# Hybrid diffusion trunk on one core: the second layer's last two modulation units from its mixer into its routing, its second gate's rows loaded during the expert blocks

## What is computed

```python
def adaln(cvec, w_ada_l, b_ada_l):
    m = jax.nn.silu(cvec) @ w_ada_l + b_ada_l
    return jnp.split(m[:, None, :], 6, axis=-1)
...
for l in range(DEPTH):
    sh1, sc1, g1, sh2, sc2, g2 = adaln(c, w_ada[l], b_ada[l])
    h = modulate(rmsnorm(xs, norm1_w[l]), sh1, sc1)
    mix = mixer_latent(h, ...)
    xs = xs + g1 * mix
    h = modulate(rmsnorm(xs, norm2_w[l]), sh2, sc2)
    xs = xs + g2 * moe_ffn(h, w_router, router_bias, w_gate[l], w_up[l], w_down[l])
```

## Time and profile before

| | us |
|---|---|
| median of three runs | 757.26 (756.87 to 758.19) |
| the profiled execution | 757.27, span 755.5, mean granted clock 0.996 |

### The profile page before, as it was taken

How to read it: one execution, slowest core, us unless ns; L and a number is a source line. 1 busy time by engine, 2 the same in 40 slices (tenths; PEclk the granted TensorE clock), 3 DMA queues, 4 the chain that set the end, 5 groups by cost and what they waited for, 6 DMA issues and landing times.

```text
span 755.5 us, 10417 instructions
## 1 busy us (share of the span) xinstructions
PE 723.2 (96%) x3950; PEld 354.8 (47%) x3950; DVE 328.2 (43%) x880; ACT 215.8 (29%) x491; POOL 141.4 (19%) x234
## 2 busy tenths in 40 slices
PE   5899999999999999999999999999999899999995
PEld 3357553346445534433344755435644653443332
DVE  2022625647635552312471253474853556231157
ACT  2210145745024101011322024574602310110132
POOL 4146032220110100101102502313011011010112
PEclk9999999999999999999999999999999999999998
DMA  8999335997208799999896233497430379999962
GB/s 315 354 325 364 113 118 194 386 377 296 113 8 349 305 414 414 423 418 424 315 387 244 92 111 119 164 387 306 175 113 14 126 316 410 422 421 421 423 251 84
DMA packets 65655, 207.95 MB, mean 275 GB/s; under 512 B 8089, under 2 KB 8961, under 8 KB 53315
## 3 DMA queue, kind: packets, MB, share of 16 engines
q1 hardware_dynamic: 54936, 179.86, 61.5%
q10 hardware_dynamic: 5547, 16.12, 5.5%
q0 software_dynamic: 5120, 11.28, 4.4%
HBM read 199.92 MB, written 12.88 MB: 282 GB/s over the span
## 4 chain that ended last, share of the span: by engine, by line
PE 77%; DVE 8%; DMA 8%; ACT 3%; issue 2%; POOL 1%; SPq 1%; POOLq 0%; ACTq 0%; DVEq 0%
PE bank L2413 15%; PE bank L2297 11%; PE bank L2040 8%; PE bank L2428 7%; PE bank L1984 6%; PE bank L2097 5%; PE bank L1905 5%; DMA arena<-in_w_up_dram 3%; PE bank L2026 3%; DMA ring<-in_w_ada_dram 2%; PE bank L2404 2%; PE bank L2142 2%; PE bank L2130 2%; DMA arena<-y_exp,y_idx 2%; PE bank L2389 1%
## 5 line engine op out<-in xcount | busy, mean ns | idle before, releaser
L2413 PE MATMUL bank<-ring,work 128*32 128x512 f32 (+1 forms) x640 | 114.2, 595 | 1.3 <-DMA arena<-in_w_up_dram 1.3
L2413 PEld LDWEIGHTS bank<-ring,work 128*32 128x32 f32 (+1 forms) x640 | 33.3, 120 | 73.1 <-issue 72.0
L1739 DVE COPY xs_tok<-bank 128x256 f32<-128x256 f32 x20 | 8.5, 424 | 134.7 <-PE bank L2420 134.7
L2428 PE MATMUL bank<-ring,xs_tok 128*64 128x512 f32 (+2 forms) x320 | 65.7, 597 | 1.0 <-DVE xs_tok L1739 1.0
L2040 PE MATMUL bank<-arena,ring 128*128 128x384 f32 x192 | 62.2, 486 | 0.0
L2413 PE MATMUL bank<-arena,work 128*64 128x512 f32 (+1 forms) x128 | 56.9, 597 | 0.0
L848 POOL DMA_INDIRECT gather_at<-h_rows,idx x18 | 18.2, 1011 | 173.1 <-PE bank L2404 130.7
L1905 PE MATMUL bank<-ring,cpad 128*32 128x512 f32 x384 | 49.7, 603 | 0.7 <-DMA ring<-in_w_ada_dram 0.7
L2040 PEld LDWEIGHTS bank<-arena,ring 128*128 128x128 f32 x192 | 36.5, 190 | 25.0
L1984 PE MATMUL bank<-ring,arena 128*128 128x512 f32 x96 | 42.8, 598 | 0.9 <-DVE arena L1281 0.6
L2297 PE MATMUL bank<-ring,arena 128*128 128x512 f32 x96 | 43.6, 597 | 0.0
(11 more groups left out here) (384 smaller groups left out, 1100.6 us busy)
## 6 DMA issues: line engine op xcount, KB each, us to landing
ring<-in_w_ada_dram SPq DMA_DIRECT2D x48, 1024.0 KB, 10.1
ring<-in_w_down_dram SPq DMA_DIRECT2D x28, 1024.0 KB, 10.6
ring<-in_w_gate_dram SPq DMA_DIRECT2D x24, 1024.0 KB, 7.2
ring<-in_w_up_dram SPq DMA_DIRECT2D x24, 1024.0 KB, 10.7
ring<-in_w_in_dram SPq DMA_DIRECT2D x15, 1024.0 KB, 14.9
ring<-in_w_out_dram SPq DMA_DIRECT2D x8, 1024.0 KB
arena<-in_w_gate_dram SPq DMA_DIRECT2D x8, 1024.0 KB
arena<-in_w_up_dram SPq DMA_DIRECT2D x8, 1024.0 KB
```

The lines of the kernel that those rows point to most:

```text
L2413: last = mm(bank[b][at:at + n, :].rearrange("p (i f) -> p i f", i=2), rows_T[:, kt * P + at:kt * P + at + n], gate_up_of(s)[:, kt, :, :], ...
L2428: last = mm(bank[5 + hf][at:at + n, :], hidT[:, b, f * P + at:f * P + at + n], w[:, f, hf * 512:(hf + 1) * 512], start=f == 0, stop=f == 1)
```

## The change

ADA_CUT gets a further cut at 22, so that group 4 of layer 1 has six units (16 to 21) and a new group 5 has units 22 and 23, which hold g2 of layer 1. ADA_GAP becomes a pair, one group for each layer's routing. In ORDER the out units of layer 1 go ahead of the two units. FILL of layer 1 loses its places (2, "end"), "states", ("scan", 0) and ("scan", 2), one half unit each. In layer 1's routing the units are put where three and four constant products were, and ada_columns where two of four were. GATES gets a third entry: in layer 1, g1 is transposed, stored and loaded ahead of the output products as before; g2 is transposed by PE behind hid_of(2), stored by ACT in block 2, and loaded in block 4, and DVE waits for it only ahead of result_gated(0). The store of layer 1's states goes ahead of moe unit 2, not of unit 4.

```diff
@@ -43,8 +43,8 @@
-ADA_CUT = (2, 4, 14, 16, 24)
-ADA_MIX, ADA_GAP = (2, 4), 3
+ADA_CUT = (2, 4, 14, 16, 22, 24)
+ADA_MIX, ADA_GAP = (2, 4), (3, 5)
 ADA_COL = [0, 2, 1, 3, *range(4, 24)]
@@ -58,8 +58,7 @@
     ORDER += [("out", OUT_U * _l + j) for j in range(OUT_U)]
-    if _l == 0:
-        ORDER += [("ada", j) for j in range(*ADA_CUT[ADA_GAP - 1:ADA_GAP + 1])]
+    ORDER += [("ada", j) for j in range(*ADA_CUT[ADA_GAP[_l] - 1:ADA_GAP[_l] + 1])]
     MOE_AT.append(len(ORDER))
@@ -293,7 +292,7 @@
         ada_part = qT[:, 1, :, :].rearrange("p a c -> p (a c)")
-        part_of = lambda i: qkv_flat[:, 0:512] if i == ADA_GAP else ada_part
+        part_of = lambda i: qkv_flat[:, 0:512] if i in ADA_GAP else ada_part
         modT = sb("modT", DEPTH, 48, 2)
@@ -308,8 +307,10 @@
         exp_at = lambda k: 4 if k == 1 else min(2 * k + 3, 24)
-        GATES = (((0, 0), (0, 1)), ((1, 0), (1, 1)))
-        gate_cols = ada_part[0:2 * KT, 0:2 * P].rearrange("r (n c) -> r n c", n=2)
+        GATES = (((0, 0), (0, 1)), ((1, 0),), ((1, 1),))
+        LAST_GATE = len(GATES) - 1
+        gate_cols = [v[0:2 * KT, 0:2 * P].rearrange("r (n c) -> r n c", n=2)
+                     for v in (ada_part, ada_part, qkv_flat[:, 2 * DM:])]
         epst = sb("epst", 4)
@@ -461,7 +462,8 @@
         ADA_BANK = 7
-        bank_of = lambda i: bank[5 if i == ADA_GAP else ADA_BANK]
+        bank_of = lambda i: bank[5 if i in ADA_GAP else ADA_BANK]
+        gates_psum = bank[ADA_BANK][0:2 * KT, 2 * P:4 * P]
         MIX_BANK = (0, 6, 6)
@@ -488,7 +490,7 @@
                  (1, 0, "after"): 1, (1, 2, "after"): 1, (1, 3, "after"): 1, (1, "end"): 1,
-                 (2, 0, "ahead"): 1, (2, 2, "ahead"): 1, (2, "end"): 1, "states": 1, ("scan", 0): 1, ("scan", 2): 1})
+                 (2, 0, "ahead"): 1, (2, 2, "ahead"): 1})
         assert [sum(_f.values()) for _f in FILL] == [ADA_PARTS * (ADA_CUT[_i] - ADA_CUT[_i - 1]) for _i in ADA_MIX]
@@ -623,7 +625,7 @@
                 for pair, k in MOE_UNITS:
-                    if (pair, k) == ((0, 1), SPLIT)[l]:
+                    if (pair, k) == ((0, 1), (1, 0))[l]:
                         states_stored(l)
@@ -955,25 +957,25 @@
-            def gates_stored(l):
-                n = len(GATES[l])
-                k = 2 * l
-                act.wait_ge(s_gt, l + 1)
-                act.activation(gate_cols[:, 0:n, :],
-                               bank[ADA_BANK][0:2 * KT, 0:n * P].rearrange("r (n c) -> r n c", n=n),
+            def gates_stored(i):
+                n = len(GATES[i])
+                act.wait_ge(s_gt, i + 1)
+                act.activation(gate_cols[i][:, 0:n, :], gates_psum[:, 0:n * P].rearrange("r (n c) -> r n c", n=n),
                                ACT.Copy).then_inc(s_gtc, 1)
-                act.wait_ge(s_gtc, l + 1)
+                act.wait_ge(s_gtc, i + 1)
+                k = 2 * GATES[i][0][0] + GATES[i][0][1]
                 for g in range(2):
-                    dma(gate_dram[k:k + n, g].rearrange("n b c -> b n c"), gate_cols[g::2, 0:n, :]).then_inc(s_gst, 16)
-            def gates_loaded(l):
+                    dma(gate_dram[k:k + n, g].rearrange("n b c -> b n c"), gate_cols[i][g::2, 0:n, :]).then_inc(s_gst, 16)
+            def gates_loaded(i):
+                l = GATES[i][0][0]
                 act.wait_ge(s_out, 16 * STORES * (l + 1))
...
                 act.wait_ge(s_yoff, 4 * (l + 1))
-                act.wait_ge(s_gst, 32 * (l + 1))
-                for w in range(2):
+                act.wait_ge(s_gst, 32 * (i + 1))
+                for _l, w in GATES[i]:
                     for g in range(2):
@@ -1130,8 +1132,7 @@
                     rows_stored(t)
-                if l == 0:
-                    ada_rows(ADA_GAP)
+                ada_rows(ADA_GAP[l])
@@ -1162,6 +1163,10 @@
                         silu(e + 1, (e + 1) % 2)
+                    if l == DEPTH - 1 and e == 2:
+                        gates_stored(LAST_GATE)
+                    if l == DEPTH - 1 and e == 4:
+                        gates_loaded(LAST_GATE)
                     if e == NB - 2:
@@ -1738,13 +1743,13 @@
-                dve.wait_ge(s_gate[1], 32 * (l + 1))
+                if l < DEPTH - 1:
+                    dve.wait_ge(s_gate[1], 32 * (l + 1))
                 one_hots(ROWS_AT, LISTS[1][1])
...
                 one_hots(*LISTS[2])
-                if l == 0:
-                    modulation(ADA_GAP)
+                modulation(ADA_GAP[l])
                 hidden(0, 0)
@@ -1762,6 +1767,8 @@
                 weighted(0)
+                if l == DEPTH - 1:
+                    dve.wait_ge(s_gate[1], 32 * (l + 1))
                 result_gated(0)
@@ -1952,12 +1959,12 @@
-            def gate_rows(l):
-                pe.wait_ge(s_mod, ADA_MIX[l] + 1)
-                for k, (ll, w) in enumerate(GATES[l]):
-                    last = tr(bank[ADA_BANK][0:2 * KT, k * P:(k + 1) * P],
-                              modT[:, ll, 24 * w + 16:24 * w + 24, :].rearrange("p b g -> p (b g)"), ident[:, :])
+            def gate_rows(i, group):
+                pe.wait_ge(s_mod, group + 1)
+                for k, (l, w) in enumerate(GATES[i]):
+                    last = tr(gates_psum[:, k * P:(k + 1) * P],
+                              modT[:, l, 24 * w + 16:24 * w + 24, :].rearrange("p b g -> p (b g)"), ident[:, :])
                 last.then_inc(s_gt, 1)
@@ -2330,7 +2337,7 @@
                 projected(0, 0)
-                gate_rows(l)
+                gate_rows(l, ADA_MIX[l])
                 y_turned(2)
@@ -2345,10 +2352,7 @@
                 pe.wait_ge(s_oc, 2 * NT * (l + 1))
-                if l == 0:
-                    ada(ADA_CUT[ADA_GAP] - 1)
-                else:
-                    clock_kept(5, 3)
+                ada(ADA_CUT[ADA_GAP[l]] - 1)
                 norm_transposes(k, 2)
@@ -2356,10 +2360,7 @@
                 back(2)
-                if l == 0:
-                    ada(ADA_CUT[ADA_GAP])
-                else:
-                    clock_kept(5, 4)
+                ada(ADA_CUT[ADA_GAP[l]])
@@ -2392,12 +2393,14 @@
                 pe.wait_ge(s_btc, 6 * l + 2)
-                clock_kept(4, 4)
+                if l == DEPTH - 1:
+                    ada_columns(ADA_GAP[l])
+                clock_kept(4, 4 if l == 0 else 2)
                 pe.wait_ge(s_btc, 6 * (l + 1))
...
                 if l == 0:
-                    ada_columns(ADA_GAP)
+                    ada_columns(ADA_GAP[l])
@@ -2451,8 +2454,8 @@
                     pe.wait_ge(s_yc, 2 * b + (2 * NB * l + 2))
-                    if l == 0 and b == 0:
-                        pe.wait_ge(s_mod, ADA_GAP + 1)
+                    if b == 0:
+                        pe.wait_ge(s_mod, ADA_GAP[l] + 1)
                     for p in pairs_of(b):
@@ -2508,6 +2511,8 @@
                     hid_of(b)
+                    if l == DEPTH - 1 and b == 2:
+                        gate_rows(LAST_GATE, ADA_GAP[l])
                     if b + 2 < NB:
```

## The result

The changed kernel took 760.17 us (median of 9 runs, 758.1 to 761.73) where the kernel before took 757.48 (9 runs, 756.78 to 759.44): a ratio of 1.0033, 95% interval 1.0023 to 1.0042. It is slower by 2.7 us. The forecast was 758.3, with a range of 755.6 to 760.4 and 0.49 for "within 0.2%". The range holds the time; the likeliest case (757.3 to 759.0) does not.

A forecast was written before the change was run, and what follows sets the result against it. PE and a gapless DMA queue were taken to run level in layer 1's expert blocks, the later setting the end. Stream start -2.05 (mixer -1.85, gate rows -0.2), gate loads +2.8, gathers +0.3: +1.05 on 757.3, so 758.3; range 755.6 to 760.4.

The forecast's parts named there:

- The mixer, -1.85: Layer 1's mixer: taking out four half units starts what follows 1.85 us earlier (bounds 1.5 and 4.0).
- the sign of being wrong in the prediction, under 1.4: Expert stream's start, forecast 2.05 us earlier: a shift of under 1.4 us, or 3 or more, would show the prediction wrong.
- The routing, 0: Layer 1's routing: two whole units replace constant products that only filled waits; cost 0 to 0.1 us, taken as 0.
- The gate loads, +2.8: Expert blocks: 1 MB of second gate loads in the full DMA queue delays unit 21 by 2.8 us (2.5 to 3.2).
- The gathers, +0.3: End of the expert stream: result gathers overlap unit 21's load by about one us, at a quarter share, costing 0.3 us.
- rival B: End of the stream: gathers collide with unit 21's load, making the landing +1.75 to +2.55 us; 759.5 us, chance 0.14.
- Equal turns: Gathers and expert loads share the DMA engines equally, not a quarter to three quarters; the overlap then costs 1.0 us.
- PE's wait, 3.8: Ahead of the last first half: PE waits 3.8 us for unit 21, in place of 0.9.
- The tail follows it: End of layer 1: DVE's tail moves by the same +1.05 us as the landing of unit 21.
- Rival C: Last first half: TensorE's clock falls in PE's new wait, half speed for 3 to 4 us, +1.7; 760.0 us, chance 0.15.
- Rival A: Expert stream: the gate loads cost nothing, PE and stream both end 2.05 us earlier; 755.2 us, chance 0.16.
- D: Rival, chance 0.05: routing cover fails, at most 1 us, 759.3. With figures near 107 to 110: stream start to last first half.

The follow-up runs named there:

- warm: The changed kernel with seven constant products put on PE ahead of its wait for unit 21; 758.82 us, ratio 1.0021 to the kernel before.
- the last one: The changed kernel with the last gate's rows made on TensorE from two bf16 parts, without DMA loads; 756.19 us, ratio 0.9977 to the kernel before.

## Why the prediction was right or wrong

**The mixer, -1.85.** Right. The first y product starts 1.77 earlier. The values product starts at 519.43, 0.35 earlier for 0.25 (the DVE copy that it needs also started 0.07 earlier). Scan 2 gives nothing, as said: from the first to the third y product it is 7.85 us before (526.42 to 534.27) and after (524.65 to 532.50). The start of the stream moved by 2.38, not 2.05. Some 0.5 of that is one operation of POOL in the same stretch which took 1.25 us in the traces of before and of the kernel without loads and 0.70 in that of after. POOL's timeline, first of before, then of after:

```profile
540.66 1.25 POOL L838 TENSOR_TENSOR grs<-gss,epst 128x2 f32<-128x2 f32 x1
```

```profile
538.89 0.70 POOL L840 TENSOR_TENSOR grs<-gss,epst 128x2 f32<-128x2 f32 x1
```

In the kernel without loads, where it took 1.25, the start moved by 1.81. Over all traces the start is a poor witness (see below the table; by the sign of being wrong in the prediction, under 1.4, three traces of kernels with the unit move would speak against it: 1.21, 1.13 and 0.37). Counted from the values product, which itself gains some 0.3, the move brings 1.5 to 2.2 more in every one of them. That agrees with the forecast; that the pair came out at 2.38 is partly the luck of the trace.

**The routing, 0.** Right: -2.32 at the output product and -2.41 behind the second routing unit.

**The gate loads, +2.8.** About right, and the mechanism is the one forecast. They were issued at 671.5 (forecast: 672). The pair of traces gives 2.96 with the gathers. Over more traces, D is 107.03, 107.32, 107.85, 107.39 and 108.14 with nothing added ahead of unit 21 (mean 107.5) and 109.99, 109.99, 109.79, 110.02 and 109.78 with both loads (mean 109.9): 2.4. The first five differ by up to 1.1 us, the other five by 0.24. That lies nearer to the bytes by 421 GB/s (2.5) than to the 2.8 by 375 GB/s, but with that scatter it does not decide between them.

**The gathers, +0.3, and rival B.** Measured 0.2, no more than the scatter of the five traces. Equal turns would have cost 1.0 or more here, and no run shows that. The Trainium skill, DMA: Bandwidth & Descriptors, Queues, rings and completion order, which I took as speaking for B, has an engine go round between its queues packet by packet. It does not say that two queues get equal shares of the bytes; that was my step. The landing of the first pair in the earlier trace rows was the better guide.

**PE's wait, 3.8.** Measured 3.6 and 3.4, and 3.8 in the kernel with the gate split alone.

**"The tail follows it."** This step failed. The sum took it that the last first half takes 7.09 us whenever unit 21 lands. It took 8.57 to 8.79, because the clock had gone down in the wait that the sum itself had forecast, or just behind it. Rival C named this, its mechanism and its price (+1.7, 760.0 us), and gave it 0.15. Measured are 1.48 and 1.70 in the two traces of the changed kernel. That price rested on 3 to 4 us at half speed, for which no row of the kernel before stood; the clock was low for some 3 to 3.5 us in the two traces. That the median, 760.17, lies so near to 760.0 is luck in part: the landing of unit 21 moved by 0.58 us where the sum had 1.05, and the trace that shows C's mechanism took 759.35. The argument against it, that the clock was at 1.00 until 2 us after PE's last product, says nothing about a wait of 3.8 us: the same rows put the fall 2 to 4 us after the end, which is inside that wait. They made C at least as likely as not. The Trainium skill, TensorE: Matmul & The Clock Gate, Part 1, has an idle array fall to half its clock, and five of the six traces here with a wait over 2 us agree.

**Rival A** (loads free) is refuted by the kernel without loads. Its own figure, 755.2, lay outside the stated range (from 755.6), a slip of the prediction. **D** (the routing's cover fails) is refuted by the routing rows.

**What the prediction lacked** besides: that the stream binds again behind unit 21. It shows in warm, where the clock is kept: PE then waits 0.9 us for unit 23.

## What to carry to other kernels

In a queue that is full to the end, bytes added were paid here at each of the three places where they were put: early they delayed the next load that PE waits for, late they delayed the gathers or the last load. Look for another engine with room that can make the data (here 1 MB of broadcast rows from some 1.8 us of TensorE, part of it inside waits).

A forecast wait of TensorE of 2 to 4 us should be priced with the work behind it at half clock as well, 1.5 to 1.7 us here in four traces of five and 3.0 behind a wait of 5.4, unless something keeps the engine busy.

Before a gain is booked on the engine that waits, ask which load it meets next.

## What the runs showed of the hardware

**TensorE's clock after a short wait.** It fell to its lower level in the traces with waits of 3.6, 3.4, 3.8 and 2.3 us, where it was back some 3 to 4 us after work had begun again, and in the one with 5.4, where that took 6 us. It stayed at 1.00 in one with 3.0, in one with 1.9 and in all with 1.0 or less. So the length of the wait alone does not decide. With half of the bytes and with the gate split alone the fall came only after PE had started again; four one-us windows of PE in the second, where it started at 717.84:

```profile
717.00:718.00 1.00, 0.16 (x2) 1.00 1.03 426
718.00:719.00 1.00, 1.00 (x6) 0.86 0.95 389
...
721.00:722.00 1.00, 1.00 (x4) 0.50 0.96 393
722.00:723.00 1.00, 1.00 (x7) 0.93 1.05 430
```

This seems to make the time of a kernel uneven from run to run: 757.75 to 761.25 for the changed kernel, 755.47 to 756.83 for the last one. That the clock is the cause of this spread is read from the mean clocks alone, and what decides in a single run stays open.

**An fp32 product of 512 columns** is two records of 0.43 to 0.47 us (0.9 in all), a bf16 one is a single record of 0.38, and four of them took 1.04, so that the next starts after 0.22. The count behind the x in a row is of records, not of products.

**A gather beside other streams.** The second result gather took 13.52 us to land when the gate rows were loaded at the same time, and 10.06 when it was issued 4 us later, with the gate rows long landed. In the kernel before, issued at 714.62 like the slow one (714.44) but with no gate rows beside it, it was there for ACT at 725.55, so within 10.9 us.
